# Two long attentions: a third score bank, maxima spread through the output banks, more probability buffers, values four steps behind

## The chip, the core and the metric

The kernel runs on one core of a Trainium2 chip. The metric is the device time of one execution in microseconds (us); lower is better. A core has a matrix engine (TensorE, PE in the profile, with its weight loads shown apart as PEld), VectorE (DVE), ScalarE (ACT), GpSimd (POOL) and SyncE (SP), which issues the DMAs. Each engine works through its own instructions in order and waits on semaphores for the others.

## What is computed

Three transformer layers on 1024 tokens of width 1024 in float32: one with a local attention and a feed-forward block, then two that attend over all tokens. The change touches only the attention cores of those two. In both there are 16 heads; the first (called gqa in the code) also has 256 context tokens as keys and as queries, the second (mla) has them as keys only.

```python
def gqa_attend(q, k, v):
    s = jnp.einsum('bqhgd,bkhd->bhgqk', q, k).astype(jnp.float32) * (GQA_HEAD_DIM ** -0.5)
    p = jax.nn.softmax(s, axis=-1).astype(v.dtype)
    return jnp.einsum('bhgqk,bkhd->bqhgd', p, v)

def mla_attend(q_nope, q_rope, k_nope, k_rope, v):
    s = (jnp.einsum('bqhd,bkhd->bhqk', q_nope, k_nope)
         + jnp.einsum('bqhr,bkr->bhqk', q_rope, k_rope)).astype(jnp.float32) * ((MLA_NOPE + MLA_ROPE) ** -0.5)
    p = jax.nn.softmax(s, axis=-1).astype(v.dtype)
    return jnp.einsum('bhqk,bkhd->bqhd', p, v)
...
    y = (o * jax.nn.silu(g)) @ p["w_out"]
```

## The kernel before

One class, `Attention`, writes the instructions of both attentions, engine by engine. The order on each engine is fixed by hand; a loop runs over pairs of heads (q = 0 and 1), with the last pair written out apart.

**Steps.** The queries of a head are cut into chunks c of 512: two for mla; for gqa two and a third of 256 (the context queries, which see the 256 context keys alone). Keys come in tiles of 128. A step k is one key tile of one chunk. A gqa head has 22 steps (10, 10 and 2), an mla head 20; `SB` counts those of two heads, `NC` the chunks. In the prediction Sk and Vk are the scores and the values of step k.

**What a step does.** TensorE computes scores transposed (keys by queries) into a score bank of the accumulation memory PSUM: two matmuls for gqa (lines 2288, 2289), three for mla. Numbers are split in a high and a low part of reduced precision, so that three cheap matmuls stand for one exact one. ScalarE takes the exponential (line 2341: `pf`) and rounds it (line 2347: the high part `ph`); GpSimd, in four steps of a head VectorE (`dve_lo`), subtracts for the low part (line 2390: `pl`); TensorE multiplies by the values (lines 2303 to 2305), into an output bank. The values run `LAG` = 3 steps behind the scores. PSUM has eight banks of 512 columns: PB[0] to PB[2] (the tensor PBX), PMX (three) and PD[0], PD[1]. Scores alternate between PB[0] and PB[1]; chunk 0 puts its output in PD[0], chunk 1 in PD[1], chunk 2 of gqa in PB[2]. Probabilities rotate through four buffers each of `pf`, `ph`, `pl`.

**Maxima.** The softmax needs the row maxima before the scores. TensorE computes untransposed scores of 128 queries against all keys in PMX (line 2258), VectorE reduces them (line 2415). PMX holds one such tile, so the next maxima matmul waits for the reduction before. When a chunk's tiles are done, a matmul with the identity turns them into a row ("spread", line 2269, into PB[2]) and VectorE writes that row into the queries' buffer (line 2423). `plan` says at which step this is queued: in gqa maxima for chunk 1 at steps 18, 0, 2, 4, for chunk 2 at 6, for the next head's chunk 0 at 10, 12, 14, 16; spreads at 8, 11 and 20. I call the maxima matmuls ahead of Sk Mk.

**The end of a chunk.** The values matrix has columns of ones, so the output bank also holds the softmax sums. ScalarE takes the logarithm (line 2357) and the exponential of its negative (line 2359), the reciprocal; VectorE multiplies (line 2434, the normalisation) and multiplies by the gate into MIX (line 2439). These are queued a number of steps after the chunk's last step, counted from `LAG`: on ScalarE `LAG+1`, `LAG+1`, `LAG+2` for the chunks 0, 1, 2 of gqa, after that step's exponential and before its rounding; on VectorE `lags` = `LAG+5`, `LAG+2`, `LAG+3`, after that step's maxima, row and low part. An instruction queued for step 22 or more stands in the next head.

Semaphores carry credits (`CR_...`), so that the first waits of a ring go through.

Of the kernel before, what the change touches and what calls it, by code (L numbers as in the profile page):

```python
# [16 lines left out]
F32 = mybir.dt.float32  # L17
R32 = mybir.dt.float32r
# [86 lines left out]
def mixed_program(nc, A, out):  # L105

    ctx = ExitStack()
    with ctx:
# [1915 lines left out]
        CR_PV2, CR_SC, CR_B, CR_E, CR_ROW2, CR_R, CR_N, CR_FIN2 = 4, 1, 2, 2, 1, 1, 4, 1  # L2024
# [11 lines left out]
        class Attention:  # L2036
# [7 lines left out]
            LAG = 3  # L2044

            def __init__(self, name, scope, chunks, keys, scale, layout, mix, first, first_maxima):
# [6 lines left out]
                self.PF = [scope.sb(f"{name}_pf{b}", [P, C]) for b in range(4)]  # L2053
                self.PH = [scope.sb(f"{name}_ph{b}", [P, C], R32) for b in range(4)]
                self.PL = [scope.sb(f"{name}_pl{b}", [P, C], R32) for b in range(4)]
# [15 lines left out]
                self.S = [PB[0], PB[1]]  # L2071
                self.BC = PB[2]
                self.FREE = self.BC if self.mla else PMX[:, 0:C]
                self.O = [PD[0], PD[1], self.BC]
# [5 lines left out]


# [19 lines left out]
                self.lags = (self.LAG + 4, self.LAG + 4, 0) if self.mla else (self.LAG + 5, self.LAG + 2, self.LAG + 3)  # L2101
# [4 lines left out]
            def tasks(self, k, last):  # L2106

                q, kk = divmod(k, self.SB // 2)
                res, n_tile = [], 0
                for step, kind, (dh, c), t in self.plan:  # L2110
                    if step == kk and not (last and q == 1 and dh):
                        n = n_tile if kind == "max" else self.last_tile[dh, c]
                        res.append((kind, (q + dh) % 2, c, t, (q + dh) * self.NC + c,
                                    len(self.ahead) + q * self.NT + n, dh + q == 2))
                    if kind == "max":
                        n_tile += 1
                return res

# [117 lines left out]
            def pe_begin(self, pe):  # L2236
# [25 lines left out]
                def bcast(i, c, g, tile):  # L2262
# [4 lines left out]
                    if NC == 3:  # L2267
                        pe.wait_ge(self.norm, i * (2 * NC) + ((g - 1) // NC * NC + CR_N))
                    pe.matmul(self.BC[0:4, 0:n], self.M[g % 2][:, 0:4], ident[:, :].unsqueeze(1).to_broadcast([P, n // P, P]),
                              start=True, stop=True).then_inc(self.bcast, 1)  # L2270

                def scores(i, k):
# [6 lines left out]
                    pe.wait_ge(self.exp, i * SB + (k - 2 + CR_E + 1))  # L2279
                    s = self.S[k % 2][:, 0:n]  # L2280
# [11 lines left out]
                def values(i, k):  # L2292
# [5 lines left out]
                    if first:  # L2298

                        pe.wait_ge(self.norm, i * (2 * NC) + (q * NC + c - NC + CR_N + 1))  # L2300
                    o = self.O[c][:, 0:n]
                    ph, pl = self.PH[k % 4][:, 0:n], self.PL[k % 4][:, 0:n]
# [21 lines left out]
                return ahead, lambda: bcast(0, 0, 0, 3), rest  # L2324
# [7 lines left out]
            def act_begin(self, act):  # L2332
# [3 lines left out]
                def probs(i, k, between):  # L2336
# [3 lines left out]
                    self.wait_lo(act, i, k - 4)  # L2340
                    act.activation(self.PF[k % 4][:, 0:n], self.S[k % 2][:, 0:n], ACT.Exp, scale=self.scale)\  # L2341
# [3 lines left out]
                    act.wait_ge(self.pv, i * SB + (k - 4 + CR_PV2 + 1))  # L2345
                    act.wait_ge(self.exp, i * SB + (k + CR_E + 1))
                    act.activation(self.PH[k % 4][:, 0:n], self.PF[k % 4][:, 0:n], ACT.Copy).then_inc(self.hi, 1)  # L2347
# [39 lines left out]
            def low(self, eng, i, k):  # L2387
                n = self.chunks[self.steps[k][1]][1]
                eng.wait_ge(self.hi, i * self.SB + (k + 1))
                eng.tensor_tensor(self.PL[k % 4][:, 0:n], self.PF[k % 4][:, 0:n], self.PH[k % 4][:, 0:n].bitcast(F32),  # L2390
# [11 lines left out]
            def dve_begin(self, dve):  # L2402
# [15 lines left out]
                def row(i, q, c, g):  # L2418
# [4 lines left out]
                    dve.tensor_tensor(dst, self.BC[0:4, 0:n].rearrange("r (m p) -> r m p", m=m),  # L2423
# [34 lines left out]
                return ahead, lambda: row(0, 0, 0, 0), rest  # L2458
# [1135 lines left out]
```

## Time and profile before

| what | us |
|---|---|
| median of 3 executions | 3427.53 (3425.10 to 3428.85) |
| the profiled execution | 3428.63 |
| its span, first to last instruction | 3426.7 |
| first long attention (gqa), about | 1779 to 2279 of the span |
| second long attention (mla), about | 2801 to 3331 of the span |
| TensorE busy over the span | 3299.4 (96%) |
| VectorE, ScalarE, GpSimd busy | 2248.3, 1729.3, 1525.9 |

A profile names for each instruction its start, its duration and the idle time of its engine before it, with what ended that idle time. A matmul's duration (0.40 us for 512 columns) overlaps with the next one; what counts is the distance of their starts. Where TensorE waited, part of the wait is listed under the weight load (PEld).

### The profile page before, as it was taken

What the parts mean: (1) busy time and instruction counts of PE and PEld (TensorE: products, weight loads), DVE (VectorE), ACT (ScalarE), POOL (GpSimd) and SP (SyncE); (2) the same over time, 40 slices, a digit from 0 to 9 for tenths busy, and PEclk for the clock granted to TensorE, in tenths of its full rate; (3) what the DMA queues carried; (4) which work ended last, traced back from release to release, by engine and by line L of the source; (5) the groups of instructions that cost most, each with busy time, mean ns of one, the idle gap of its engine ahead of it and who ended that gap; (6) DMA issues with size and microseconds to landing.
All of it is one profiled execution on the core that took longest, in us unless ns stands there. A gap on an engine that the chain in (4) does not pass through costs nothing.

```text
span 3426.7 us, 47942 instructions
## 1 busy us (share of the span) xinstructions
PE 3299.4 (96%) x14993; PEld 2638.9 (77%) x14993; DVE 2248.3 (66%) x2647; ACT 1729.3 (50%) x2959; POOL 1525.9 (45%) x962
## 2 busy tenths in 40 slices
PE   7999999999999999999999999999988989999999
PEld 5778878778888888778877777778765668888877
DVE  6685878677576675648627777767557876666661
ACT  3343878432010111334328898871455558888880
POOL 2402444644444445520037777767210026666653
PEclk9999999999999999999999999999999999999999
DMA  3134232411212122122354344413254344232312
GB/s 104 43 123 131 62 84 56 154 50 57 91 48 94 49 74 73 42 85 107 120 137 94 80 102 99 95 62 111 102 212 150 123 121 133 56 80 66 74 37 80
DMA packets 196089, 313.57 MB, mean 92 GB/s; under 512 B 100928, under 2 KB 111680, under 8 KB 195968
## 3 DMA queue, kind: packets, MB, share of 16 engines
q1 hardware_dynamic: 195968, 312.01, 31.5%
q8 instruction: 70, 1.15, 0.1%
q14 instruction: 51, 0.42, 0.0%
HBM read 234.02 MB, written 77.92 MB: 91 GB/s over the span
## 4 chain that ended last, share of the span: by engine, by line
PE 66%; POOL 10%; DVE 9%; issue 9%; ACT 4%; DMA 2%; SPq 0%; POOLq 0%; DVEq 0%; ACTq 0%
PE PBX L284 10%; PE PBX L285 10%; PE PBX L286 10%; POOL gqa_pl L2390 8%; PE PMX L284 4%; PE PMX L285 4%; PE PMX L286 4%; PE PMX L2258 2%; PE PD L2303 2%; PE PD L2304 2%; PE PD L2305 2%; PE PBX L2285 2%; PE PBX L2286 2%; PE PBX L2284 2%; PE PD L1035 2%
## 5 line engine op out<-in xcount | busy, mean ns | idle before, releaser
L217 POOL TENSOR_TENSOR w_hi<-w_stage,zero 128x1024 fp32r<-128x1024 f32 (+2 forms) x116 | 225.5, 1944 | 1150.1 <-PE PBX L286 730.5
L2390 POOL TENSOR_TENSOR gqa_pl<-gqa_pf,gqa_ph 128x512 fp32r<-128x512 f32 (+1 forms) x288 | 369.3, 1299 | 144.2 <-ACT gqa_ph L2347 142.5
L2390 POOL TENSOR_TENSOR mla_pl<-mla_pf,mla_ph 128x512 fp32r<-128x512 f32 x256 | 339.6, 1332 | 206.5 <-ACT mla_ph L2347 200.2
L2415 DVE TENSOR_REDUCE mla_m<-PMX 128x1 fp32r<-128x1280 f32 x128 | 190.9, 1491 | 176.7 <-PE PMX L2258 176.6
L219 POOL TENSOR_TENSOR w_lo<-w_stage,w_hi 128x1024 fp32r<-128x1024 f32 (+2 forms) x116 | 293.2, 2527 | 9.1
L2415 DVE TENSOR_REDUCE gqa_m<-PMX 128x1 fp32r<-128x1280 f32 x144 | 201.6, 1400 | 138.5 <-PE PMX L2258 137.6
L1929 ACT ACTIVATE conv_in<-PBX 128x512 f32<-128x512 f32 x66 | 39.6, 601 | 478.8 <-PE PBX L286 474.8
L2341 ACT ACTIVATE mla_pf<-PBX 128x512 f32<-128x512 f32 x320 | 190.8, 596 | 92.2 <-PE PBX L2286 75.6
L2341 ACT ACTIVATE gqa_pf<-PBX 128x512 f32<-128x512 f32 (+1 forms) x352 | 200.9, 571 | 42.4 <-PE PBX L2289 38.7
L2347 ACT ACTIVATE gqa_ph<-gqa_pf 128x512 fp32r<-128x512 f32 (+1 forms) x352 | 215.2, 611 | 12.4 <-PE PD L2305 0.4
L284 PE MATMUL PBX<-ffn_hi,w_hi 128*128 128x512 f32 x528 | 206.9, 392 | 4.7 <-DVE ffn_lo L711 4.7
L2347 ACT ACTIVATE mla_ph<-mla_pf 128x512 fp32r<-128x512 f32 x320 | 202.0, 631 | 11.4
L286 PE MATMUL PBX<-ffn_hi,w_lo 128*128 128x512 f32 x528 | 205.5, 389 | 0.0
L285 PE MATMUL PBX<-ffn_lo,w_hi 128*128 128x512 f32 x528 | 205.5, 389 | 0.0
L1958 DVE SCALAR_TENSOR_TENSOR conv_out<-conv_in,VEC,conv_out 128x1024 f32<-128x1024 f32 x88 | 188.0, 2136 | 12.8 <-DVE conv_out L1958 0.6
L284 PE MATMUL PBX<-l_hi,w_hi 128*128 128x512 f32 (+1 forms) x400 | 157.3, 393 | 8.6 <-DVE l_lo L711 6.8
L479 DVE SCALAR_TENSOR_TENSOR PMX<-mod_w,cond_s 128x1024 f32<-128x1024 f32 x96 | 158.2, 1648 | 5.7 <-DVE PMX L479 0.9
L1954 DVE TENSOR_SCALAR conv_out<-conv_in,VEC 128x1024 f32<-128x1024 f32 x44 | 73.1, 1661 | 134.6 <-ACT conv_in L1929 133.8
L1642 POOL TENSOR_TENSOR swa_pl<-swa_pf,swa_ph 128x512 fp32r<-128x512 f32 x64 | 81.6, 1276 | 156.3 <-ACT swa_ph L1567 156.0
L285 PE MATMUL PBX<-l_lo,w_hi 128*128 128x512 f32 (+1 forms) x400 | 144.0, 360 | 0.0
L286 PE MATMUL PBX<-l_hi,w_lo 128*128 128x512 f32 (+1 forms) x400 | 143.9, 360 | 0.0
L284 PE MATMUL PBX<-h_hi,w_hi 128*128 128x512 f32 x336 | 136.7, 407 | 4.0 <-issue 1.2
(524 smaller groups left out, 9874.9 us busy)
## 6 DMA issues: line engine op xcount, KB each, us to landing
mod_w<-in_w_mod SPq DMA_DIRECT2D x48, 512.0 KB, 3.5
w_stage<-in_w_up SPq DMA_DIRECT2D x44, 512.0 KB, 3.5
w_stage<-in_w_go SPq DMA_DIRECT2D x24, 512.0 KB, 3.8
gqa_k<-kh_d SPq DMA_DIRECT2D x32, 320.0 KB, 4.8
gqa_q<-qh_d SPq DMA_DIRECT2D x32, 320.0 KB, 6.7
w_stage<-in_w_down SPq DMA_DIRECT2D x24, 384.0 KB, 3.1
qh_d<-heads_qh SPq DMA_DIRECT2D x32, 256.0 KB, 2.1
ql_d<-heads_ql SPq DMA_DIRECT2D x32, 256.0 KB, 2.3
```

What stands on the lines that cost most here:

```text
L217: pool.tensor_tensor(w_hi[s][:, 0:st.cols], w_stage[s][:, 0:st.cols], z, ALU.add).then_inc(w_hi_done, 1)
L219: pool.tensor_tensor(w_lo[s][:, 0:st.cols], w_stage[s][:, 0:st.cols], w_hi[s][:, 0:st.cols].bitcast(F32), ALU.subtract).then_inc(w_split, 1)
L284: pe.matmul(ps, wh, xh, start=first, stop=False)
L285: pe.matmul(ps, wh, xl, start=False, stop=False)
L286: return pe.matmul(ps, wl, xh, start=False, stop=last)
L479: dve.scalar_tensor_tensor(out=PMX[:, C:3 * C], in0=bufs[s], scalar=1.0, in1=conds[j], op0=ALU.mult, op1=ALU.mult, accum_out=MOD[:, bass.d ...
L1642: pool.tensor_tensor(swa_PL[K % 4][:, :, 0:m], swa_PF[K % 2][:, :, 0:m], swa_PH[K % 4][:, :, 0:m].bitcast(F32), ALU.subtract).then_inc(a1[ ...
L1958: dve.scalar_tensor_tensor(out=y, in0=CU[s][:, j:j + S], scalar=w(j), in1=y, op0=ALU.mult, op1=ALU.add).then_inc(conv_step, 1)
L2341: act.activation(self.PF[k % 4][:, 0:n], self.S[k % 2][:, 0:n], ACT.Exp, scale=self.scale)\
L2347: act.activation(self.PH[k % 4][:, 0:n], self.PF[k % 4][:, 0:n], ACT.Copy).then_inc(self.hi, 1)
L2390: eng.tensor_tensor(self.PL[k % 4][:, 0:n], self.PF[k % 4][:, 0:n], self.PH[k % 4][:, 0:n].bitcast(F32), ALU.subtract).then_inc(self.lo_dv ...
L2415: dve.tensor_reduce(self.M[g % 2][:, t:t + n], PMX[:, 0:n * w].rearrange("p (n w) -> p n w", n=n), AX.X, ALU.max, negate=True).then_inc(se ...
```

## The change

- `LAG` goes from 3 to 4, so the values of step k are queued after the scores of step k+4. Everything that is counted from `LAG` moves one step later with it: ScalarE's reciprocals, VectorE's normalisations. For mla one of the two numbers in `lags` is lowered by one, so its chunk 1 keeps its step.
- Scores rotate through PB[0], PB[1], PB[2]: in mla in all steps but two at each head's end, in gqa in steps 8 to 19; in the other gqa steps two banks are used, since PB[2] holds chunk 2's output. New: `ring`, `s_of`, `s_back`.
- The spread of the maxima goes to the output bank that is idle then (`spread`: PD[0] for chunk 0, PD[1] otherwise; the very first of all still to PB[2]), and waits until that bank's last output has been normalised. In gqa the scores of chunk 1 begin only when all outputs of the head before are normalised, and its values only when chunk 2's row has been written.
- Probability buffers: six for gqa and five for mla, instead of four (`p_of`, `p_back`).

```diff
-        CR_PV2, CR_SC, CR_B, CR_E, CR_ROW2, CR_R, CR_N, CR_FIN2 = 4, 1, 2, 2, 1, 1, 4, 1
+        CR_PV2, CR_SC, CR_B, CR_E, CR_ROW2, CR_R, CR_N, CR_FIN2 = 6, 1, 2, 3, 1, 1, 4, 1
...
-            LAG = 3
+            LAG = 4
...
-                self.PF = [scope.sb(f"{name}_pf{b}", [P, C]) for b in range(4)]
+                buffers = 5 if self.mla else 6
+                self.PF = [scope.sb(f"{name}_pf{b}", [P, C]) for b in range(buffers)]
...
-                self.S = [PB[0], PB[1]]
-                self.BC = PB[2]
-                self.FREE = self.BC if self.mla else PMX[:, 0:C]
-                self.O = [PD[0], PD[1], self.BC]
+                self.S = PB
+                self.FREE = PB[2] if self.mla else PMX[:, 0:C]
+                self.O = [PD[0], PD[1], PB[2]]
...
+                self.s_of, self.s_back = self.ring([3] * 6 + [2] if self.mla else [2] * 4 + [3] * 4 + [2], CR_E)
+                self.p_of, self.p_back = self.ring([5] * 4 if self.mla else [6, 6, 5, 5], CR_PV2)
...
-                self.lags = (self.LAG + 4, self.LAG + 4, 0) if self.mla else (self.LAG + 5, self.LAG + 2, self.LAG + 3)
+                self.lags = (self.LAG + 4, self.LAG + 3, 0) if self.mla else (self.LAG + 5, self.LAG + 2, self.LAG + 3)
...
+            def ring(self, turns, most):
+
+                of = [b for n in turns * 2 for b in range(n)]
+                back = [next(d for d in range(1, self.SB) if of[k - d] == of[k]) for k in range(self.SB)]
+                return of, [min(d, most) for d in back]
+
+            def spread(self, c, first):
+
+                return PB[2] if first else self.O[min(c, 1)]
...
-                    if NC == 3:
-                        pe.wait_ge(self.norm, i * (2 * NC) + ((g - 1) // NC * NC + CR_N))
-                    pe.matmul(self.BC[0:4, 0:n], self.M[g % 2][:, 0:4], ident[:, :].unsqueeze(1).to_broadcast([P, n // P, P]),
+                    if not first:
+                        pe.wait_ge(self.norm, i * (2 * NC) + (g - c // 2 - NC + CR_N + 1))
+                    pe.matmul(self.spread(c, first)[0:4, 0:n], self.M[g % 2][:, 0:4], ident[:, :].unsqueeze(1).to_broadcast([P, n // P, P]),
...
-                    pe.wait_ge(self.exp, i * SB + (k - 2 + CR_E + 1))
-                    s = self.S[k % 2][:, 0:n]
+                    if first and c == 1 and NC == 3:
+
+                        pe.wait_ge(self.norm, i * (2 * NC) + (q * NC + CR_N))
+                    pe.wait_ge(self.exp, i * SB + (k - self.s_back[k] + CR_E + 1))
+                    s = self.S[self.s_of[k]][:, 0:n]
...
+                    if first and c == 1 and NC == 3:
+
+                        pe.wait_ge(self.row_done, i * (2 * NC) + (q * NC + 2 + CR_ROW2 + 1))
...
-                    self.wait_lo(act, i, k - 4)
-                    act.activation(self.PF[k % 4][:, 0:n], self.S[k % 2][:, 0:n], ACT.Exp, scale=self.scale)\
+                    self.wait_lo(act, i, k - self.p_back[k])
+                    act.activation(self.PF[self.p_of[k]][:, 0:n], self.S[self.s_of[k]][:, 0:n], ACT.Exp, scale=self.scale)\
                        .then_inc(self.exp, 1)
                     between()
 
-                    act.wait_ge(self.pv, i * SB + (k - 4 + CR_PV2 + 1))
+                    act.wait_ge(self.pv, i * SB + (k - self.p_back[k] + CR_PV2 + 1))
```

Where instructions stand in a row shows the moves. In the rows, REGISTER_ALU computes what the next wait compares with, and is left out where "..." stands. Line numbers after the change are some 20 higher.

ScalarE, opening of a gqa head. Before: from step 0's exponential (gqa_pf) on; gqa_ph is the rounding, gqa_rd the reciprocal of chunk 1 (from PD) of the head before.

```order
L2341 ACTIVATE gqa_pf<-PBX 128x512
L2346 REGISTER_ALU
L2347 ACTIVATE gqa_ph<-gqa_pf 128x512
L2155 REGISTER_ALU
L2341 ACTIVATE gqa_pf<-PBX 128x512
L2356 REGISTER_ALU
L2357 ACTIVATE gqa_rd<-PD 64x512
L2358 REGISTER_ALU
L2359 ACTIVATE gqa_rd<-gqa_rd 64x512
```

After, the same stretch:

```order
L2359 ACTIVATE gqa_pf<-PBX 128x512
L2364 REGISTER_ALU
L2366 ACTIVATE gqa_ph<-gqa_pf 128x512
L2167 REGISTER_ALU
L2359 ACTIVATE gqa_pf<-PBX 128x512
L2364 REGISTER_ALU
L2366 ACTIVATE gqa_ph<-gqa_pf 128x512
L2167 REGISTER_ALU
L2359 ACTIVATE gqa_pf<-PBX 128x512
L2375 REGISTER_ALU
L2376 ACTIVATE gqa_rd<-PD 64x512
```

The reciprocal of chunk 1 stood behind the exponential of step 1, and stands now behind that of step 2.

VectorE, opening of a gqa head. Before: the maxima of step 2 (gqa_m), normalisation (gqa_t) and gate multiply (MIX) of chunk 1, the maxima of step 4, chunk 2's normalisation (from PBX) and gate, the maxima of step 6 (128x2).

```order
L2415 TENSOR_REDUCE gqa_m<-PMX 128x1
...
L2434 TENSOR_TENSOR gqa_t<-PD,gqa_rd 64x512
...
L2439 TENSOR_TENSOR MIX<-gqa_t,gqa_gate 64x512
...
L2415 TENSOR_REDUCE gqa_m<-PMX 128x1
...
L2434 TENSOR_TENSOR gqa_t<-PBX,gqa_rd 64x256
...
L2439 TENSOR_TENSOR MIX<-gqa_t,gqa_gate 64x256
...
L2415 TENSOR_REDUCE gqa_m<-PMX 128x2
```

After:

```order
L2435 TENSOR_REDUCE gqa_m<-PMX 128x1
...
L2454 TENSOR_TENSOR gqa_t<-PD,gqa_rd 64x512
...
L2459 TENSOR_TENSOR MIX<-gqa_t,gqa_gate 64x512
...
L2435 TENSOR_REDUCE gqa_m<-PMX 128x1
...
L2435 TENSOR_REDUCE gqa_m<-PMX 128x2
...
L2454 TENSOR_TENSOR gqa_t<-PBX,gqa_rd 64x256
```

Chunk 1's work keeps its place between the maxima of steps 2 and 4; chunk 2's has gone behind those of step 6.

VectorE, end of a gqa head. Before: the maxima of step 16, normalisation and gate of chunk 0, the maxima of step 18, the next head's row (gqa_q).

```order
L2415 TENSOR_REDUCE gqa_m<-PMX 128x1
...
L2434 TENSOR_TENSOR gqa_t<-PD,gqa_rd 64x512
...
L2439 TENSOR_TENSOR MIX<-gqa_t,gqa_gate 64x512
...
L2415 TENSOR_REDUCE gqa_m<-PMX 128x1
...
L2423 TENSOR_TENSOR gqa_q<-PBX,ident_f 4x512
```

After:

```order
L2435 TENSOR_REDUCE gqa_m<-PMX 128x1
...
L2435 TENSOR_REDUCE gqa_m<-PMX 128x1
...
L2454 TENSOR_TENSOR gqa_t<-PD,gqa_rd 64x512
...
L2459 TENSOR_TENSOR MIX<-gqa_t,gqa_gate 64x512
...
L2443 TENSOR_TENSOR gqa_q<-PD,ident_f 4x512
```

Chunk 0's normalisation has moved behind the maxima of step 18, and the row is read from PD[0].

## Rows read from the trace of the kernel before

**Rows 1.** Busy time by stretch: stretch, length, then each engine's busy us (instructions), clock, DMA.
```profile
1779.00:2279.00 500.00, 490.70 (x2196) 382.27 (x2195) 353.17 (x345) 442.57 (x798) 368.55 (x287) 1.00 0.42 89
2801.00:3331.00 530.00, 527.18 (x2313) 425.33 (x2312) 327.97 (x292) 424.62 (x704) 338.31 (x255) 1.00 0.34 78
```

**Rows 2.** Waits in the first attention: who waited for whom, us in total, times, longest.
```profile
PEld PD L2303 <- POOL gqa_pl L2390: 27.7, 66, 0.7
...
PE PMX L2258 <- DMA gqa_v<-vl_d: 2.8, 1, 2.8
```

**Rows 3.** Timeline, TensorE, one gqa head: start us, duration, instruction, [idle before].
```profile
2030.84 0.40 PE L2288 MATMUL PBX<-gqa_q,gqa_k 128*128 128x512 f32 x1
...
2037.62 0.40 PE L2289 MATMUL PBX<-gqa_q,gqa_k 68*128 68x512 f32 x1
2038.29 0.50 PE L2303 MATMUL PD<-gqa_ph,gqa_v 128*128 128x512 f32 x1 [0.27 <-POOL gqa_pl L2390]
...
2039.09 0.40 PE L2258 MATMUL PMX<-gqa_k,gqa_q 128*128 128x256 f32 x2
...
2040.73 0.39 PE L2289 MATMUL PBX<-gqa_q,gqa_k 68*128 68x512 f32 x1
2041.18 0.50 PE L2303 MATMUL PD<-gqa_ph,gqa_v 128*128 128x512 f32 x1
...
2044.54 0.74 PE L2258 MATMUL PMX<-gqa_k,gqa_q 128*128 128x512 f32 x3
2045.11 0.40 PE L2288 MATMUL PBX<-gqa_q,gqa_k 128*128 128x512 f32 x1
...
2059.19 0.40 PE L2269 MATMUL PBX<-ident,gqa_m 128*4 128x512 f32 x1
...
2060.64 0.50 PE L2303 MATMUL PD<-gqa_ph,gqa_v 128*128 128x512 f32 x1
2060.98 0.40 PE L2304 MATMUL PD<-gqa_ph,gqa_v 128*128 128x512 f32 x1
...
2062.03 0.40 PE L2288 MATMUL PBX<-gqa_q,gqa_k 128*128 128x512 f32 x1
...
2093.06 0.39 PE L2288 MATMUL PBX<-gqa_q,gqa_k 128*128 128x512 f32 x1
```

**Rows 4.** Timeline, ScalarE, opening of the same head.
```profile
2031.59 0.60 ACT L2341 ACTIVATE gqa_pf<-PBX 128x512 f32<-128x512 f32 x1 [1.06 <-PE PBX L2289]
...
2032.77 0.60 ACT L2341 ACTIVATE gqa_pf<-PBX 128x512 f32<-128x512 f32 x1
2033.39 0.60 ACT L2357 ACTIVATE gqa_rd<-PD 64x512 f32<-64x512 f32 x1
2034.02 0.63 ACT L2359 ACTIVATE gqa_rd<-gqa_rd 64x512 f32<-64x512 f32 x1
...
2035.20 0.60 ACT L2341 ACTIVATE gqa_pf<-PBX 128x512 f32<-128x512 f32 x1
...
2037.52 0.58 ACT L2341 ACTIVATE gqa_pf<-PBX 128x512 f32<-128x512 f32 x1
...
2039.50 0.60 ACT L2341 ACTIVATE gqa_pf<-PBX 128x512 f32<-128x512 f32 x1
```

**Rows 5.** Timeline, VectorE, the same head: opening, step 10, end.
```profile
2035.15 0.68 DVE L2434 TENSOR_TENSOR gqa_t<-PD,gqa_rd 64x512 f32<-64x512 f32 x1
...
2037.12 1.49 DVE L2415 TENSOR_REDUCE gqa_m<-PMX 128x1 fp32r<-128x1280 f32 x1
...
2045.31 1.49 DVE L2415 TENSOR_REDUCE gqa_m<-PMX 128x1 fp32r<-128x1280 f32 x1 [1.14 <-PE PMX L2258]
...
2055.55 0.67 DVE L2434 TENSOR_TENSOR gqa_t<-PD,gqa_rd 64x512 f32<-64x512 f32 x1
```

**Rows 6.** Timeline, an mla head: chunk 1's normalisation on VectorE, the spread on TensorE.
```profile
2980.71 0.67 DVE L2434 TENSOR_TENSOR mla_t<-PD,mla_rd 64x512 f32<-64x512 f32 x1
...
2981.90 0.39 PE L2269 MATMUL PBX<-ident,mla_m 128*4 128x512 f32 x1
```

## What I expect, and how the numbers follow

> **What bounds the kernel now.** Read the busy table by stretch first [rows 1]. The two long attentions are 1030 of the 3426.7 us, and in both the TensorE is busy nearly all the time: 527.2 of 530 us in the second, 490.7 of 500 us in the first. Busy hides short stalls, so the waits come next [rows 2]: in the first attention the weight load for the values (PD, line 2303) stood 27.7 us behind GpSimd's low halves, in 66 places. In the second attention that wait hardly exists, so the change has nothing to win there, and at most 2.8 us of idle time. Third, the timeline of one head of the first attention, the one that begins at 2030.84 [rows 3]. I write S7, V7 for the scores and values of key step 7 of 22 (steps 0 to 9 are query chunk 0, 10 to 19 chunk 1, 20 and 21 the short chunk 2), M6 for the maxima issued ahead of S6, and times from the head's S0. The head takes 31.19 us, the next one 31.03, so 31.11 on average. Back to back, 1280 columns take 0.57 us (2044.54 to 2045.11), so 512 take 0.23 and a full step (two scores, three values) 1.17.
>
> The stalls are in fixed places. V2 starts 0.67 us after the matmul before it, where 0.23 is the pitch, and its second matmul 0.34 later: the weights of a matmul that had to wait are not loaded under the one before, which costs a further 0.10. Together 0.54. V4 is late by 0.22 plus that 0.10. V18's second matmul stands 0.34 behind its first, 0.10 again, with some 0.04 before it. V1 loses about 0.2 of the same 27.7.
>
> **What the change does to those.** Values one step later give the low halves one more step, 1.17 us, where V2 was 0.44 late; five or six probability buffers let ScalarE go on. All these value stalls should go: about 1.1 us per head (0.54, 0.32 in this head and less in the next, which is 0.16 shorter, 0.14 and 0.2). 15 heads at 1.1 would be 16 us, if nothing else came late. But two other things are late next, and both come from one detail: the work at the end of a query chunk is counted from the same lag. The reciprocal of chunk 1 (logarithm, then exponential, on ScalarE) moves from after the exponential of step 1 to after that of step 2; the normalisation of chunk 0 on VectorE moves behind the maxima of step 18, and that of chunk 2 behind those of step 6.
>
> **ScalarE at the head's opening.** Now [rows 4] the exponential of step 0 begins at 0.75, 0.75 after S0, of step 1 at 1.93, the reciprocal's two instructions at 2.55 and 3.18, the exponential of step 2 at 4.36: from step 1 on without idle time, because the reciprocal fills the time in which the TensorE does M2. In the changed kernel step 2's exponential stands ahead of the reciprocal and needs S2. S2 starts at 0.47 + 0.70 (S0, V18) + 0.47 + 0.70 (S1, V19, now a full value step) + 0.57 (M2) = 2.91. So the exponential starts at 2.91 + 0.75 = 3.66, with ScalarE idle from 3.09, the logarithm 0.62 later at 4.28, the exponential of the reciprocal 0.63 later at 4.91, done at 5.54. Before it was done at 3.81.
>
> **VectorE behind it.** VectorE works strictly in its order: maxima of step 2, normalisation and gate of chunk 1, maxima of step 4. Now [rows 5] the normalisation starts at 4.31, when the maxima of step 2 are done, half a microsecond after the reciprocal, and the maxima of step 4 start 1.97 later, at 6.28, ending at 7.77. The TensorE's M6 writes the same three PMX banks and waits for that end. It comes at 8.25, so it doesn't wait, but only because V1, V2 and V4's like had held the TensorE: by pitch alone it would have come at 7.5. In the changed kernel the normalisation can't start before 5.54 + 0.05 = 5.59. Plus 1.97 the maxima of step 4 start at 7.56 and end at 9.05. M6 goes at 9.1, and 0.10 is lost on its weights: 9.2, against the 7.5 to 8.0 at which the TensorE arrives. **This is the new wait**, about 1.2 to 1.7 us per head. Queued behind M6 on the TensorE is everything: S6, V2 and all that follows; nothing can pass.
>
> Apart from this the Trainium skill has a sentence on it (Perfetto Trace Analysis, section Tensor Engine Instruction): only the TensorE's queue may pull a weight load ahead, and the others are strict FIFO. That agrees with the order in which VectorE stands in these rows; without it a maxima instruction could pass the waiting normalisation and this wait would not exist.
>
> **The rest of the head.** From M6 to S10 it is 6.02 us now (2039.09 to 2045.11), of which V4's lateness is 0.32: 5.70. S10 at 9.22 + 5.70 = 14.92, against 14.27 now. ScalarE doesn't hold this stretch: step 2 at 3.66, plus 1.26 for the reciprocal and 1.16 a step as two steps take 2.32, puts step 4 at 7.24; 1.16 to step 5, and 1.98 from 5 to 6 with chunk 2's reciprocal between, gives step 6 at 10.38, done by 11.0, before S8 (12.0) wants its bank. From S10 to the next head 16.92 less V18's 0.14 is 16.78: 31.70.
>
> One more wait is new: the maxima of the next head's chunk 0 are spread in PD[0], and this waits for the normalisation of chunk 0. The spreading matmul (2059.19) stands 14.08 after S10. M18 is 0.57 + 2 x 1.17 = 2.90 ahead of it, at 11.18; its reduction starts 0.77 later (as 2044.54 to 2045.31 [rows 3, 5]), takes 1.49, and only then comes the normalisation of 0.68: 14.12, plus 0.05 for the signal. The spread waits 0.1 and its weights a little: 0.15. Today the normalisation is ahead of that reduction and 3.0 us early. The head: **31.85**.
>
> **The sum**, against the profiled execution's 3428.6 us (span 3426.7): 14 steady heads (second to fifteenth) by 31.85 - 31.11 = 0.74: +10.4. The first head has no chunk behind it and gets the 0.15 alone. It also stands still for 2.8 us for the second head's loads [rows 2], whose landing the change doesn't move: 0, with 0.7 (one value step more left to do afterwards) as upper bound. In the last head no maxima follow step 6 and ScalarE sets the pace; its idle time before step 2's exponential, 3.09 to 3.66, comes through at most whole: 0 to 0.6, I take 0.3. Both other moves (row_done ahead of V10, the normalised output ahead of S10) are signals given microseconds earlier and cost nothing while VectorE is under 2 us late there. The third score bank itself and the larger buffers add no instruction. The second attention: heads have slack on VectorE. Its normalisation starts at 2980.71, takes 0.67, and the spread that will now wait for it is at 2981.90 [rows 6]: 0.5 us to spare; the shorter lag chosen there keeps its place in the queue. 0, bounds -0.8 to +2. Sum +10.9: 3439.5 for the profiled execution, which lay 1.1 over the median 3427.5. So 3438 us for the median. By the uncertain terms (0.2 us per head either way, and the ends) 3434 to 3443.
>
> **Rivals.** A: *the waits simply go.* If the reciprocal were in time and M6 did not wait, every value stall would be won: 15 x 1.1 = 16 us, 3411. For it: the stalls in [rows 2] name GpSimd and nothing else, and the cure fits. Against: the queue order on VectorE and the reciprocal, 1.7 us later. The Trainium skill (Perfetto Trace Analysis, section Optimization Strategy) says that the same gap repeating on the engine that should be saturated can mean too few buffers; by that rule more banks and buffers bring this rival's 3411. This is the case on the faster side, and it decides if M6 finds its reduction done by 7.5.
>
> B: *ScalarE only.* The VectorE chain turns out 1.3 us shorter than I make it (a shorter gate multiply, no TensorE effect), and what is left is two score banks in steps 0 to 9. Step 3's exponential starts at 6.08 and ends at 6.68, so S5 waits from 6.3 to 6.7 and loses 0.5; S8 waits for step 6 (done 11.0) instead of going at 10.8 and loses 0.35. The head is 30.0 by pitch plus 0.85: 30.85, 14 x 0.26 = 3.6 us less: 3424. This is within 0.2%, as would be anything with M6 waiting only half as long.
>
> C: *the second attention suffers too.* Its spread waits for a normalisation 0.5 us ahead of it. If that came 0.8 us later, 0.3 + 0.1 by 30 chunks would be +12 on top of the forecast: 3450. Nothing moves it there, so this is unlikely.
>
> D: *the change doesn't act in the first attention*: the lag is the same constant for both, and the order of the queues shows it moved. No chance of its own.
>
> **Chances.** Forecast 0.60 (3434 to 3443), B and its mixtures with the forecast 0.26 (3421 to 3434), A 0.11, C 0.03. 0.2% or 7 us is about what a measurement of this kernel can tell from no change; so faster by more (under 3420.7) 0.12, within 0.27, slower (over 3434.4) 0.61. The range 3422 to 3444 leaves out A and C and a rest.
>
> **What would show it.** In the changed trace of the first attention: waits of the TensorE's weight load for GpSimd's gqa_pl under 3 us; instead a wait of the PMX matmuls for VectorE's gqa_m, some 15 times and 1 us or more each; VectorE's gqa_t waiting for ScalarE's gqa_rd about 15 times by 1 us (now none for the 512-wide ones); ScalarE idle 0.5 us before step 2's exponential; a head of 31.7 to 31.9 us, S10 at 14.9. Heads of the second attention within 0.1 us of today's. I am wrong in the main step if M6 doesn't wait for VectorE, and wrong in size if the gate multiply between normalisation and maxima is not the 1.1 us of this head.

## The result: 0.56% slower, and the profile after

| what | before | after |
|---|---|---|
| median (us) | 3427.53 | 3447.26 |
| runs | 5, 3425.10 to 3431.85 | 5, 3442.74 to 3450.34 |
| the profiled execution | 3428.63 | 3443.37 |
| its span | 3426.7 | 3441.4 |
| ratio of the times | | 1.0056, interval 1.0044 to 1.0067 |

The change costs 19.7 us; 10.9 were forecast, and 3447 lies above the range (3422 to 3444). To see where the time went I cut the span at the first score matmul of each head:

| us | before | after | forecast for the difference |
|---|---|---|---|
| ahead of the first gqa head | 1778.3 | 1774.7 | 0 |
| first gqa head | 35.0 | 35.6 | 0.15 |
| mean of the 14 steady gqa heads | 31.10 | 32.39 | 0.74 |
| last gqa head | 31.8 | 31.9 | 0.3 |
| between the attentions | 519.9 | 521.6 | 0 |
| all mla heads (a steady one 33.10 in both) | 533.0 | 530.7 | 0 |
| behind them | 93.4 | 93.4 | 0 |

The 14 steady heads cost 14 x 1.29 = 18.1 us. The stretch ahead of gqa, the one between the attentions and the start of mla move by a few microseconds between the profiles of this study (1774.6 to 1783.0 ahead of gqa), so this single profile, 3.9 us under the median of its kernel, says nothing on them. What is to be explained is 1.29 us per head where 0.74 was forecast.

The waits of the changed kernel in the first attention (waiting engine, tile and line, then whom it waited for; us in total, times, longest; these sums take in the first and the last head as well):

```profile
PE PMX L2270 <- DVE gqa_m L2435: 20.4, 16, 1.4
...
PEld PMX L2270 <- DVE gqa_m L2435: 30.4, 25, 1.8
PEld PBX L2303 <- ACT gqa_pf L2359: 7.6, 16, 0.5
PEld PD L2281 <- DVE gqa_t L2454: 4.6, 14, 0.4
...
DVE gqa_t L2454 <- ACT gqa_rd L2378: 16.0, 16, 1.1
```

Against [rows 2]: the 27.7 us behind GpSimd's `gqa_pl` are gone entirely. In their place stands the wait of the maxima matmul for VectorE's reduction, 16 times and up to 1.4 us on the matmul itself. VectorE in turn waits for the reciprocal, 16 times by 1 us.

The busy table of the same stretch (length, then PE, PEld, DVE, ACT, POOL, clock, DMA share, GB/s), to be held against [rows 1]:

```profile
1779.00:2289.00 510.00, 485.75 (x2168) 380.45 (x2169) 350.17 (x341) 437.59 (x782) 355.45 (x282) 1.00 0.41 87
```

TensorE is busy 485.75 of 510 us, where it was 490.70 of 500. The granted clock rounds to 1.00 in both, the 2.4 GHz level. Only the first head has a short stretch at the lower level, in both kernels: behind the wait for the second head's loads, the granted clock of that head's 35 us is 0.95 before and after. The steady heads of these two profiles have none, so the clock has no part in the 1.29 us.

The timeline of one steady head of the changed kernel, S0 at 2037.14. First ScalarE (answers to [rows 4]), with start, duration, instruction and idle time before:

```profile
2039.15 0.58 ACT L2359 ACTIVATE gqa_pf<-PBX 128x512 f32<-128x512 f32 x1
...
2040.88 0.60 ACT L2359 ACTIVATE gqa_pf<-PBX 128x512 f32<-128x512 f32 x1 [0.48 <-PE PBX L2304]
2041.50 0.59 ACT L2376 ACTIVATE gqa_rd<-PD 64x512 f32<-64x512 f32 x1
2042.12 0.63 ACT L2378 ACTIVATE gqa_rd<-gqa_rd 64x512 f32<-64x512 f32 x1
```

ScalarE stands idle for 0.48 us until S2 is there, and only then come step 2's exponential (3.74 after S0; forecast 3.66) and the reciprocal (its exponential at 4.98; forecast 4.91). Next VectorE (answers to [rows 5]):

```profile
2040.33 1.49 DVE L2435 TENSOR_REDUCE gqa_m<-PMX 128x1 fp32r<-128x1280 f32 x1 [1.20 <-PE PMX L2270]
2042.79 0.68 DVE L2454 TENSOR_TENSOR gqa_t<-PD,gqa_rd 64x512 f32<-64x512 f32 x1 [0.97 <-ACT gqa_rd L2378]
2043.61 1.58 DVE L2459 TENSOR_TENSOR MIX<-gqa_t,gqa_gate 64x512 f32 x1
2045.23 1.49 DVE L2435 TENSOR_REDUCE gqa_m<-PMX 128x1 fp32r<-128x1280 f32 x1
```

The normalisation starts at 5.65 (forecast 5.59). But the gate multiply takes 1.58 us. In the kernel before, in the head of [rows 5], it stood between the two rows shown there and took 1.11:

```profile
2035.98 1.11 DVE L2439 TENSOR_TENSOR MIX<-gqa_t,gqa_gate 64x512 f32 x1
```

The sum's 1.97 from normalisation to reduction holds this 1.11. The reduction now starts at 8.09 instead of 7.56. Last TensorE (answers to [rows 3]), M6, S6 and the next head's first scores:

```profile
2044.98 0.39 PE L2323 MATMUL PD<-gqa_pl,gqa_v 128*128 128x512 f32 x1
2046.77 0.50 PE L2270 MATMUL PMX<-gqa_k,gqa_q 128*128 128x256 f32 x2 [1.40 <-DVE gqa_m L2435]
2047.11 0.40 PE L2303 MATMUL PBX<-gqa_q,gqa_k 128*128 128x512 f32 x1
...
2069.48 0.50 PE L2303 MATMUL PBX<-gqa_q,gqa_k 128*128 128x512 f32 x1
```

M6 starts at 9.63 instead of 9.1, after 1.40 us of idle time, and the head is 32.34 long.

### The profile page after: what moved, and what is told of

The parts are those of the page before. It is cut to its first block, busy times and chain, and to the rows that moved or that the text cites. A ratio compares the mean times of both kernels' runs of the same rounds, so it can differ in the third digit from the quotient of the medians.

```text
span 3441.4 us, 47970 instructions
## 1 busy us (share of the span) xinstructions
PE 3299.3 (96%) x14993; PEld 2640.8 (77%) x14993; DVE 2227.4 (65%) x2647; ACT 1729.8 (50%) x2959; POOL 1523.5 (44%) x962
## 4 chain that ended last, share of the span: by engine, by line
PE 76%; DVE 10%; issue 5%; ACT 4%; POOL 2%; DMA 2%; SPq 0%; DVEq 0%; ACTq 0%; POOLq 0%
PE PBX L284 10%; PE PBX L285 10%; PE PBX L286 10%; PE PMX L284 4%; PE PMX L285 4%; PE PMX L286 4%; PE PMX L2270 4%; PE PD L2322 4%; PE PD L2321 4%; PE PD L2323 4%; PE PBX L2300 2%; PE PBX L2301 2%; PE PBX L2299 2%; PE PD L1035 2%; PE PBX L2303 2%
```

## The experiments

My theory after the result: the late reciprocal holds VectorE's reduction and so M6, as forecast, and the surplus is the gate multiply, which now meets a whole GpSimd instruction. The rivals: something else in the change (the third bank, the spreads, the values' lag) costs time as well; or the end of chunk 0 does. All times below are device times against the kernel before on the same chip. "Head" is the mean of the 14 steady gqa heads.

**1. Chunk 1's reciprocal where it was**, the rest as changed.

```diff
-                lags, lag = (self.LAG + 1, self.LAG + 1, self.LAG + 2), ...
+                lags, lag = (self.LAG + 1, self.LAG + 1, 0) if self.mla else (self.LAG + 1, self.LAG + 0, self.LAG + 2), ...
```

> The changed kernel with one number different: on ScalarE the reciprocal of chunk 1 of the first attention is queued behind step 1's exponential again (LAG + 0 instead of LAG + 1). Everything else of the change stays. My theory (the late reciprocal makes VectorE's normalisation and the maxima reduction behind it late, and the TensorE waits at M6): the normalisation starts at 4.7 to 4.9 after S0 instead of 5.64, the reduction of step 4 at 6.4 to 6.7 instead of 8.09, M6 goes near 8.0 instead of 9.63, and a head takes 30.8 to 31.2 us instead of 32.40: about 3421 to 3428 us. Rival (the spreads in the output banks with their new waits, or the banks and buffers themselves, cost the time): the head stays within 0.3 us of 32.4 and the time near 3443 to 3447.

3422.0 us, ratio 0.9980 (0.9971 to 0.9990); the head 30.66, or 1.73 less than in the changed kernel. One number in one queue turns 0.56% slower into 0.20% faster. M6 goes at 8.00. So the reciprocal's place carries the loss, and the rest of the change, taken together, is a gain.

**2. The ends of all three chunks where they were** (ScalarE's reciprocals and VectorE's normalisations), with lag 4, banks, spreads and buffers as changed.

```diff
-                self.lags = ... (self.LAG + 5, self.LAG + 2, self.LAG + 3)
+                self.lags = ... (self.LAG + 4, self.LAG + 2, self.LAG + 2)
...
-                lags, lag = (self.LAG + 1, self.LAG + 1, self.LAG + 2), ...
+                lags, lag = ... (self.LAG + 0, self.LAG + 0, self.LAG + 1), ...
```

> The changed kernel with all three ends of a chunk of the first attention queued at the steps that they had before the change (ScalarE LAG, LAG, LAG + 1; VectorE LAG + 4, LAG + 2, LAG + 2 with LAG = 4). Values four steps behind, banks and buffers as changed. My theory: besides what the reciprocal of chunk 1 gives, the 0.1 us wait of the spread at step 20 and the lateness of the next head's M2 (about 0.2) go, so the head takes 30.6 to 31.0 us and the kernel 3418 to 3424 us, faster than before the change by up to 0.25%. What then remains over 30.0 is S5 and S8 waiting for ScalarE's exponentials. Rival A of the prediction (without late chunk ends all stalls go): 30.0 us a head, 3411 us. Rival (banks, buffers or new waits cost the time): near 3443.

3421.1 us, ratio 0.9982 (0.9973 to 0.9991); the head 30.55, so chunks 0 and 2 give 0.1 us more than chunk 1 alone, no difference in the time of the kernel. M6 goes at 7.89. The gain is 0.55 us a head, not the 1.1 that the value stalls had measured. What is left stands in ScalarE's timeline, from the head's opening (S0 at 2029.34):

```profile
2033.76 0.60 ACT L2359 ACTIVATE gqa_pf<-PBX 128x512 f32<-128x512 f32 x1
2034.38 0.64 ACT L2366 ACTIVATE gqa_ph<-gqa_pf 128x512 fp32r<-128x512 f32 x1
2034.92 0.58 ACT L2359 ACTIVATE gqa_pf<-PBX 128x512 f32<-128x512 f32 x1
2035.54 0.63 ACT L2366 ACTIVATE gqa_ph<-gqa_pf 128x512 fp32r<-128x512 f32 x1
2036.07 0.58 ACT L2359 ACTIVATE gqa_pf<-PBX 128x512 f32<-128x512 f32 x1
2036.68 0.38 ACT L2376 ACTIVATE gqa_rd<-PBX 64x256 f32<-64x256 f32 x1
```

No row has idle time in front: ScalarE runs through from step 1 on, with the two reciprocals (some 2 us) among the exponentials, and the scores wait for their bank. From the waits of the first attention in this run:

```profile
PEld PBX L2303 <- ACT gqa_pf L2359: 6.6, 24, 0.5
...
PEld PD L2321 <- POOL gqa_pl L2410: 2.5, 5, 0.7
```

The kernel before waited 2.0 us in 5 places for the exponentials, and 27.7 for the low halves. This is rival B's mechanism.

**3. The late ends alone**: the kernel before (lag 3, two banks, four buffers) with only the queue places that the change brings.

```diff
-                self.lags = ... (self.LAG + 5, self.LAG + 2, self.LAG + 3)
+                self.lags = ... (self.LAG + 6, self.LAG + 3, self.LAG + 4)
...
-                lags, lag = (self.LAG + 1, self.LAG + 1, self.LAG + 2), ...
+                lags, lag = ... (self.LAG + 2, self.LAG + 2, self.LAG + 3), ...
```

> The kernel before, with nothing of the change except that the ends of a chunk of the first attention are queued one step later on ScalarE and VectorE, as the change does to them: values three steps behind, two score banks, four buffers. My theory: the lateness is the whole cost and needs nothing of the rest: head 31.9 to 32.4 us instead of 31.11, 3438 to 3446 us, with the TensorE waiting for VectorE's gqa_m at M6 in every head. Rival (the cost lies in banks, buffers or the waits of the spreads): unchanged within 0.2%, 3424 to 3431 us.

3445.1 us, ratio 1.0051 (1.0036 to 1.0067); the head 32.16. This alone brings nearly the whole loss. VectorE in the head with S0 at 2038.96, and TensorE's M6:

```profile
2044.44 0.69 DVE L2434 TENSOR_TENSOR gqa_t<-PD,gqa_rd 64x512 f32<-64x512 f32 x1 [0.96 <-ACT gqa_rd L2359]
2045.27 1.58 DVE L2439 TENSOR_TENSOR MIX<-gqa_t,gqa_gate 64x512 f32 x1
2046.88 1.49 DVE L2415 TENSOR_REDUCE gqa_m<-PMX 128x1 fp32r<-128x1280 f32 x1
```

```profile
2048.42 0.50 PE L2258 MATMUL PMX<-gqa_k,gqa_q 128*128 128x256 f32 x2 [1.11 <-DVE gqa_m L2415]
```

The same chain, with the same 1.58 us multiply, in a kernel that has nothing else of the change.

**4. The gate multiply behind the reduction**: the changed kernel, where chunk 1's gate multiply is queued one step later, behind the maxima of step 4. The reciprocal stays late.

```diff
+                self.gate_lags = self.lags if self.mla else (self.LAG + 5, self.LAG + 3, self.LAG + 3)
...
+                def both(i, k):
+                    self.ended(final, i, k, self.lags)
+                    self.ended(gated, i, k, self.gate_lags)
```

> The changed kernel, with the gate multiply of chunk 1 in the first attention queued one step later on VectorE, behind the maxima reduction of step 4 instead of ahead of it (the normalisation stays ahead). The reciprocal is as late as in the changed kernel. The step of my sum that was off is the gate multiply: 1.58 us here against the 1.11 that I took. My theory: the reduction starts 0.7 us after the normalisation, at 6.4 instead of 8.09, M6 goes at 7.9 to 8.1, and the head takes 30.9 to 31.4 us, 3422 to 3431 us, though the reciprocal is untouched. Rival (the lateness of the reciprocal costs by another way than the reduction of step 4, for instance through the output bank): the head stays over 32.0 us.

3430.7 us, ratio 1.0010 (1.0000 to 1.0019); the head 31.15, or 1.24 less than in the changed kernel. With the multiply out of the way the reduction starts at 6.35 and M6 goes at 8.08. The normalisation still waits for the reciprocal, at 5.63. So most of what the late reciprocal costs, it costs through the multiply that stands between it and the reduction.

**5. The multiply behind the reduction, with the ends back** (experiments 2 and 4 together; the edits are theirs).

> As e2 (the changed kernel with all three chunk ends of the first attention at their old steps), and the gate multiply of chunk 1 queued behind the reduction of step 4. My theory: in e2 M6 (7.89) still waits for that reduction (6.34 to 7.83), where by pitch it would go at 7.5; with the 0.86 us gate multiply out of its way this wait goes, S8 then waits for step 6's exponential, and the head takes 30.2 to 30.5 us instead of 30.55: 3414 to 3421 us. Rival (ScalarE alone sets this stretch already): 30.5 to 30.6 us a head, 3419 to 3423.

3420.1 us, ratio 0.9978 (0.9969 to 0.9987); the head 30.55, as in experiment 2. M6 goes at 7.66 instead of 7.89, yet S8 starts at 10.88 where it was at 10.87: the time is handed to the wait for ScalarE. VectorE is no longer the limit there.

**6. Banks, spreads and buffers without the lag**: the changed kernel with three steps between scores and values.

```diff
-            LAG = 4
+            LAG = 3
...
-                self.lags = (self.LAG + 4, self.LAG + 3, 0) if self.mla ...
+                self.lags = (self.LAG + 4, self.LAG + 4, 0) if self.mla ...
```

> The changed kernel with LAG = 3, so values three steps behind and every chunk end where it was, but with three score banks, spreads in the output banks and five or six buffers. My theory: these neither cost nor win much: the value stalls at V1, V2 (about 0.75 us a head) stay, the spreads' new waits are covered: head 30.9 to 31.2 us, 3422 to 3430 us. Rival (banks or new waits cost): over 3434. Rival (the banks are what wins in e1 and e2): 30.6 us a head, 3419 to 3422.

3427.8 us, ratio 0.9995 (0.9986 to 1.0005); the head 31.08 against 31.10. Its main wait in the first attention is that of the kernel before, 27.7 in 66 places in [rows 2]:

```profile
PEld PD L2321 <- POOL gqa_pl L2410: 27.5, 65, 1.0
```

More banks and buffers do nothing for it, and cost nothing. In the first attention experiment 2 has the same order and buffers and only the fourth step of lag besides, and there 2.5 us of this wait are left. The low half is late because the order asks for it three steps behind, not because a buffer is missing. Whether lag 4 would have done with fewer than six buffers was not run. The Trainium skill (Perfetto Trace Analysis, section Optimization Strategy) reads a gap that repeats on the engine that should be saturated as a possible lack of buffers. Here that was not the cause: with more of them 27.5 of the 27.7 us stayed.

**7. Two score banks only**, as experiment 2 otherwise.

```diff
-                self.s_of, self.s_back = self.ring([3] * 6 + [2] if self.mla else [2] * 4 + [3] * 4 + [2], CR_E)
+                self.s_of, self.s_back = self.ring([2] * 10 if self.mla else [2] * 11, CR_E)
```

> As e2, but scores rotate through two banks only in both attentions (values four steps behind, six and five buffers and spreads in the output banks as in the change). My theory: the lag and the buffers win, the third bank does nothing, since the first attention's waits lie in steps 0 to 9, which use two banks in any case, and the second attention waits for nothing: head 30.5 to 30.7 us and 33.1 us, 3419 to 3424 us, as e2. Rival (the third bank carries part of the gain): head over 30.8 us.

3420.4 us, ratio 0.9974 (0.9965 to 0.9983); the head 30.56. The third bank brings nothing that can be measured, in either attention. In gqa it is used in steps 8 to 19, while in experiment 2 the longest wait of the scores for ScalarE stands at S7 (0.23 us in the head shown, 0.37 in the one before it), where chunk 2's output has the bank.

**8. A small low half in step 2.** This measures the disputed term by itself. The changed kernel, in which GpSimd's subtraction of step 2 covers 16 columns instead of 512, so that no GpSimd instruction runs when the gate multiply starts. The third values matmul of that step takes the high part instead. TensorE's work is the same, but the result leaves out the low part of one step.

```diff
+                    if not self.mla and k % 22 == 2:
+                        pl = ph
...
-                n = self.chunks[self.steps[k][1]][1]
+                n = 16 if not self.mla and k % 22 == 2 else self.chunks[self.steps[k][1]][1]
```

> The changed kernel, where in the first attention GpSimd's low part of step 2 covers 16 columns instead of 512, and the third values matmul of that step takes the high part again in its place (this leaves out the low part of one step in each head; the TensorE's work is the same). It takes away what I hold to stretch the gate multiply of chunk 1: GpSimd's instruction that runs when it starts. My theory: the multiply takes 0.69 to 0.75 us instead of 1.58, the reduction of step 4 starts at 7.2 instead of 8.09, M6 goes at 8.7 to 8.9 and the head takes 31.3 to 31.7 us instead of 32.40: 3429 to 3437 us. Rival (the multiply is long for another reason, such as where its operands lie): it stays at 1.5 us or more, and the head at 32.4.

3433.7 us, ratio 1.0018 (1.0008 to 1.0028); the head 31.55. VectorE in the head with S0 at 2035.84, and GpSimd next to it:

```profile
2041.47 0.68 DVE L2456 TENSOR_TENSOR gqa_t<-PD,gqa_rd 64x512 f32<-64x512 f32 x1 [0.97 <-ACT gqa_rd L2380]
2042.30 0.69 DVE L2461 TENSOR_TENSOR MIX<-gqa_t,gqa_gate 64x512 f32 x1
2043.02 1.49 DVE L2437 TENSOR_REDUCE gqa_m<-PMX 128x1 fp32r<-128x1280 f32 x1
```

```profile
2042.04 0.22 POOL L2412 TENSOR_TENSOR gqa_pl<-gqa_pf,gqa_ph 128x16 fp32r<-128x16 f32 x1 [1.47 <-ACT gqa_ph L2368]
2043.32 2.52 POOL L2412 TENSOR_TENSOR gqa_pl<-gqa_pf,gqa_ph 128x512 fp32r<-128x512 f32 x2 [1.06 <-ACT gqa_ph L2368]
```

The same multiply, started at the same place (6.46 after S0), takes 0.69 us and not 1.58; M6 goes 0.91 earlier, at 8.72, and the mean head is 0.84 shorter. The normalisation, which reads PSUM and one SBUF tensor, takes 0.68 in both. ScalarE's exponentials and reciprocal stand where they stood in the changed kernel to within 0.02 us, so what had held VectorE is the GpSimd instruction.

**9. Chunk 0's normalisation back** ahead of the maxima of step 18, the rest as changed (one execution).

```diff
-                self.lags = ... (self.LAG + 5, self.LAG + 2, self.LAG + 3)
+                self.lags = ... (self.LAG + 4, self.LAG + 2, self.LAG + 3)
```

> The changed kernel with only chunk 0's normalisation and gate multiply of the first attention back ahead of the maxima of step 18 on VectorE. My theory: it carries the lateness at a head's end that my sum took for 0.15 and that goes on into the next head (row, low part of step 19, the reduction of step 0, M2): the spread at step 20 and M2 wait no longer, and the head takes 32.0 to 32.2 us instead of 32.40. Rival (nothing follows from it, since M6 has slack to take it up): 32.35 to 32.45.

The mean of the 14 steady heads is 32.28 against 32.39, but it mixes two kinds. Twelve of them take 31.98 to 32.00 and 32.12 to 32.14 us by turns, 32.06 on average, which is what the theory gave. Two take 33.67 and 33.64, and in both TensorE's granted clock fell behind M6. The busy table of that stretch in one of them, and of the same stretch in the head with S0 at 2035.74, which is undisturbed:

```profile
2109.50:2114.00 4.50, 4.50 (x14) 3.48 (x15) 1.65 (x3) 2.93 (x6) 3.24 (x3) 0.62 0.94 149
2045.60:2050.00 4.40, 4.40 (x21) 3.50 (x20) 3.03 (x5) 3.88 (x7) 3.05 (x3) 1.00 0.97 182
```

A matmul of 512 columns shows 0.63 us there instead of 0.40, at the 1.2 GHz level, and each of the two heads loses 1.5 us by it. TensorE had waited 1.37 us at M6 just before, but it waits 1.26 to 1.36 there in undisturbed heads too, so the rows don't say why the clock fell in these two. The changed kernel has no such head among its 14. Undisturbed heads compared, the end of chunk 0 costs 32.39 - 32.06 = 0.33 us a head. The single time, 3447.4, can't show that.

**10. Chunk 2's end four steps later**, on top of experiment 5: chunk 2's reciprocal, its normalisation and its gate multiply leave the stretch in which ScalarE sets the pace.

```diff
-                self.lags = ... (self.LAG + 4, self.LAG + 2, self.LAG + 2)
+                self.lags = ... (self.LAG + 4, self.LAG + 2, self.LAG + 6)
...
-                lags, lag = ... (self.LAG + 0, self.LAG + 0, self.LAG + 1), ...
+                lags, lag = ... (self.LAG + 0, self.LAG + 0, self.LAG + 5), ...
```

> As e5, and chunk 2's reciprocal queued four steps later on ScalarE (behind step 8's exponential instead of step 4's), its normalisation behind step 9's place on VectorE. My theory: in steps 2 to 9 ScalarE works without idle time and S8 waits for it; taking the 0.75 us of this reciprocal out of that stretch lets S8 go at its pitch: head 30.0 to 30.3 us, 3411 to 3418 us. Rival (moving it costs as much at its new place, or the scores of step 10 then wait for the late normalisation): head 30.5 us or more.

3429.5 us, ratio 1.0000 (0.9990 to 1.0010); the head 31.16, so worse than experiment 5 by 0.6. S10 does come earlier (13.54, in experiment 2 it was 13.76). Then VectorE has chunk 2's work ahead of step 10's reduction, and the next maxima matmul waits for it (S0 at 2029.13):

```profile
2040.58 1.59 DVE L2411 TENSOR_TENSOR gqa_pl<-gqa_pf,gqa_ph 128x512 fp32r<-128x512 f32 x1
2042.20 0.42 DVE L2455 TENSOR_TENSOR gqa_t<-PBX,gqa_rd 64x256 f32<-64x256 f32 x1
2042.76 1.29 DVE L2466 TENSOR_TENSOR MIX<-gqa_t,gqa_gate 64x256 f32 x1
2044.09 1.49 DVE L2436 TENSOR_REDUCE gqa_m<-PMX 128x1 fp32r<-128x1280 f32 x1
```

```profile
2045.63 0.85 PE L2271 MATMUL PMX<-gqa_k,gqa_q 128*128 128x512 f32 x3 [0.24 <-DVE gqa_m L2436]
```

Both neighbours are again stretched by GpSimd: the low part takes 1.59 us (0.69 undisturbed), and the multiply of 256 columns, 0.42 us in the head of [rows 5] before the change, takes 1.29. Where VectorE has maxima every two steps, it has no room for them.

## Why the prediction was right in kind and wrong in size

**The chain held, step by step.** Times after S0 in the head shown:

| step of the forecast | forecast | measured |
|---|---|---|
| exponential of step 2 | 3.66 | 3.74 |
| ScalarE idle ahead of it | 0.57 | 0.48 |
| reciprocal's exponential | 4.91 | 4.98 |
| normalisation of chunk 1 | 5.59 | 5.65 |
| normalisation to reduction | 1.97 | 2.44 |
| reduction of step 4 | 7.56 | 8.09 |
| M6 | 9.1 | 9.63 |
| S10 | 14.92 | 15.44 |
| S10 to the next head | 16.93 | 16.90 |
| the head | 31.85 | 32.34 |

The direction, the place of the new wait (M6 for VectorE), its cause (the reciprocal behind step 2's exponential), the disappearance of every value stall and the untouched second attention came as forecast. Rival A fell with M6's wait, and C with mla heads of 33.10 us in both kernels. B's mechanism was real, but hidden under the larger wait: experiments 1, 2 and 5 uncover it, with a head of 30.55 to 30.66 where B had 30.85.

**The step that failed is "plus 1.97 the maxima of step 4 start".** It took the gate multiply's 1.11 us from one row of the kernel before, as if it were a property of the instruction. It is a property of where it stands. In the head of each kernel (times after S0):

| kernel | multiply starts | GpSimd's instruction ends | multiply ends | it took |
|---|---|---|---|---|
| before | 5.13 | 5.70 | 6.24 | 1.11 |
| after | 6.47 | 7.50 | 8.05 | 1.58 |
| experiment 1 | 5.57 | 5.87 | 6.42 | 0.85 |
| experiment 2 | 5.45 | 5.76 | 6.31 | 0.86 |
| experiment 4 | 7.87 | 8.77 | 9.32 | 1.45 |
| experiment 8 | 6.46 | 6.42 | 7.15 | 0.69 |

Wherever GpSimd is at work when the multiply starts, the multiply ends about 0.55 us after GpSimd's instruction does. In the changed kernel the two are tied together. The rounding of step 2, which releases GpSimd, and the reciprocal's exponential, which releases VectorE, stand next to each other on ScalarE, and GpSimd starts 0.26 us ahead of the multiply in one head of each pair, 0.35 in the other. So the multiply always meets nearly a whole GpSimd instruction. In the kernel before it met the last 0.57 of one. The row was right for its own phase, and the change moved the phase. In this head 0.47 of the 0.49 that it was off is this term. In the other head of a pair the multiply takes 1.48, or 0.37 more than the sum had. The steady heads were off by 32.39 - 31.85 = 0.54 on average, 14 times, or 7.6 us; the multiply is 14 x 0.42 = 5.9 of them.

**A second term stood at nothing: what the end of chunk 0 does to the next head.** It was given 0.15, for the spread. That was right: from S10 to the next head it is 16.90 and 16.91 us in the changed kernel and 16.78 and 16.77 in experiment 9, where this normalisation is back. But the normalisation, a gate multiply of up to 1.77 us and the row also end later than before and reach over into the next head. There VectorE's first reduction starts 0.5 or 1.0 us after S0 by turns (0.3 and 0.2 in experiment 9). M2 waits for it, so S2 starts at 2.98 or 3.21 instead of the forecast 2.91, which experiment 9 has (2.90 and 2.91). The reciprocal and the normalisation follow S2. This is 0.07 or 0.30 us a head, 0.19 on average, 14 x 0.19 = 2.7 of the 7.6 us. In experiment 1, without the late reciprocal, it is gone again by S10 (13.83 and 13.66, against 13.76 and 13.78 in experiment 2). The multiply and this term come to 0.42 + 0.19 = 0.61 where 0.54 was missing; the difference, 0.07, lies in small terms of the sum.

**The first head** was taken at 0.15 with 0.7 as upper bound, and is 0.7 longer in this pair of profiles. Its wait for the second head's loads grew from 2.8 to 3.7 us, and both profiles have the lower clock behind it. In the twelve profiles the first head takes 33.4 to 35.6 us, so one pair says little on this term.

**The range** reached 3444 because the forecast's own spread was put at 0.2 us per head, with the multiply at its one value. The other end stood in the timeline of the same head, in chunk 0's multiply, which [rows 5] leaves out:

```profile
2056.46 1.70 DVE L2439 TENSOR_TENSOR MIX<-gqa_t,gqa_gate 64x512 f32 x1 [0.24 <-DVE gqa_t L2434]
```

The same instruction, 1.70 us against 1.11, is the sign that its duration has a cause outside it. With both ends in the range, 0.59 more per head or 14 x 0.59 = 8.3 us, the upper end would have been 3444 + 8 = 3452.

What the change could have brought is experiment 5 or 7: 3420, 0.2% under the kernel before and 0.8% under the changed one. Lag 4 with the chunk ends kept in their queue places (experiment 2, 3421.1) gives it all within the noise: the intervals of experiments 2, 5 and 7 overlap. A kernel with the edits of both 5 and 7 was not run.

## What to carry to other kernels

When a constant such as a pipeline's lag is changed, list everything that is counted from it: here the lag itself won 0.55 us a head, and what was tied to it lost 1.8, of which the reciprocal one step later on ScalarE is 1.7. Don't carry the duration of a VectorE instruction with two SBUF inputs from one place to another: look up what GpSimd runs at the new place, and take the time from GpSimd's end. And before giving a stalled engine more buffers, see whether the stall is the order's: more banks and buffers alone moved nothing. Before a mean over like stretches is read, look at them one by one: two heads with a lower clock hid two thirds of what experiment 9 had to show.

## What the runs showed of the hardware

**VectorE's multiply is held by GpSimd.** A `TENSOR_TENSOR` of 64x512 that reads two SBUF tensors takes 0.69 us alone (experiment 8) and up to 1.78 with GpSimd's subtraction (1.29 us) beside it. In the traces of the kernel before, the changed one and experiment 2, 31 of 32 such multiplies end 0.54 to 0.56 us after the GpSimd instruction that ran when they started; the last one meets none and takes 0.69. The normalisation of the same size, with one input from PSUM, takes 0.67 to 0.69 in all twelve traces, also where it starts under a GpSimd subtraction (30 of 32 in experiment 2). GpSimd pays too: in the changed kernel its subtraction ahead of the multiply and the one behind show together as

```profile
2043.35 2.97 POOL L2410 TENSOR_TENSOR gqa_pl<-gqa_pf,gqa_ph 128x512 fp32r<-128x512 f32 x2 [1.49 <-ACT gqa_ph L2366]
```

which is 1.29 for the first and 1.68 for the second, the one that starts while the multiply is under way. The Trainium skill (SBUF — State Buffer, section Who interferes with whom) states that a VectorE instruction with two SBUF inputs contends with a GpSimd instruction that reads SBUF. By the summary at the end of the same page (section Summary: rules for kernel authors) the second of the two to issue is fully blocked until the first is done. The traces agree, with 0.55 us left of the multiply's 0.69 once GpSimd is done, and with GpSimd's next instruction longer by 0.39. The 0.69 multiply of experiment 8 is the case without contention.

**TensorE's clock can fall in single heads.** In experiment 9 the granted clock was 0.62 over 4.5 us of one head and 1.00 over the like stretch of others, and 512 columns took 0.63 us by the profile instead of 0.40. It cost 1.5 us each time.
